# One ScalarE table set for logarithm and exponential in a hybrid RWKV / SSD / attention backbone

## The chip, the cores and the metric

The kernel runs on one core of one Trainium2 chip. The time is the device time of one execution, in microseconds (us), and the figure for a kernel is the median over its runs. Engines are named as in the profile: PE is TensorE (PEld its weight loads), DVE is VectorE, ACT is ScalarE, POOL is GpSimd, SP is SyncE, which here only issues transfers. ACT computes a function by a table. The tables come in sets, one set is active at a time, and an instruction ACT_TABLE_LOAD makes another set the active one. A set holds several functions; if a function's set is not the active one, the compiler puts a load in front of the ACTIVATE that needs it.

## The reference, cut to what matters

Four layers over 256 context tokens and 256 latent tokens of width 1024. Layers 0 and 3 mix tokens by a bidirectional RWKV-7 scan, layer 1 by a bidirectional Mamba-2 SSD scan, layer 2 by windowed attention; each is followed by a gated convolutional FFN. All is float32.

```python
def rmsnorm(x, g, eps=NORM_EPS):
    xf = x.astype(jnp.float32)
    xf = xf * lax.rsqrt(jnp.mean(xf * xf, axis=-1, keepdims=True) + eps)
    return (xf * g.astype(jnp.float32)).astype(x.dtype)

for i in range(DEPTH):
    hl, hc = modulate(xl, norm1_g[i], ...), modulate(xc, norm1_g[i], ...)
    yc, yl = mixer(hc, hl, ...)             # rwkv, ssd, attention, rwkv
    xl = xl + ml[2] * yl                    # the same for xc, except after the last layer
    xl = xl + ml[5] * conv_ffn(modulate(xl, norm2_g[i], ...), ...)
return rmsnorm(xl, final_g)
```

A root of the form rsqrt(m + eps) is wanted at nine places: before every mixer (n10, n11, n12, n13 in the kernel), before every FFN (n20 to n23), and once at the end (nf). Inside the mixers there are more: in SSD one per group of 256 channels (`group_rmsnorm`, 8 groups), in RWKV two per tile of 128 channels (8 tiles in each of the two layers), one that makes the key a unit vector (`kkf * rsqrt(sum(kkf * kkf) + 1e-12)`) and one in the head norm of the output. SSD and RWKV need plain exponentials besides (decays), SSD and the FFN need SiLU, RWKV needs sigmoid.

## The kernel before

Each engine has its own program, and semaphores tie them. ACT has no reciprocal root that is used here: every root is exp(-0.5 ln(m + eps)), an ACTIVATE with Ln and one with Exp.
The order of work on each engine is the order in which the program is written; nothing reorders it later. The stages that the change touches:

- Norms taken by halves of the tokens (`half_norm_act`, L659 to L674; tags n20, n11, n21, n12, n22, n23). PE computes the mean square of the first half (L588, L591) while it still ends the second half of the stage before. ACT takes the root (L669 Ln, L670 Exp), DVE multiplies X by it (L681), ACT or DVE scale and shift (L673, L683) into H, and PE goes on with the next stage's products on H (L649, or L884 in the FFN). Then all again for the second half, with `table(act, LOGS)` in front.
- Norms in one piece (`inverse_root`, L714 to L717): n10 at the very start, n13 before layer 3, nf at the end. DVE L775 (L748 in nf) and ACT L734 follow, and before an RWKV layer DVE L782 and L785, which form the token-shift mixes that PE L258 multiplies.
- The start of an FFN: after n2x, DVE forms differences of token halves (L988 to L991) and sums of weight blocks (L1004 to L1007), and PE L884 multiplies them.
- SSD, 8 groups: per group ACT loads EXPS (L2078), takes exponentials of the decays (L2059, L2055, L2042), then the root of the group before (`scale`, L2062 to L2066), more exponentials, loads SILUS and does convolutions' SiLU (L2008). DVE L2205 applies the root. POOL multiplies by the decays (L1807, L1813).
- RWKV, 8 tiles: in a long list of small 64x64 products on PE (L2419), copies out of PSUM are made by ACT (L2676) and DVE (L2981, L2989). Between them `slot_steps` places the next tile's element work: "TS" loads the sigmoid set, "L01" and "L23" are the sigmoids, "TL" loads LOGS, "KS" is the Ln for the key, "TE" loads EXPS, "KE" the Exp for the key; "P2" (L2783, Ln) and "P2e" (L2786, Exp) are the root of the head norm of an earlier tile.

Of the kernel before, what the change touches and what calls it, by code (L numbers as in the profile page):

```python
# [35 lines left out]
ORDER_Q = [[0, 1, 2, 3, 4, 5, 6, 7], [3, 2, 1, 0, 7, 6, 5, 4]]  # L36
LEVELS = (2, 4, 8, 16, 32)

EXPS, SIGMOIDS, LOGS, SILUS = 0, 2, 5, 18  # L39
HEADS = 16  # L40
SSD_IN = 6208
INNER = 2048
# [91 lines left out]
def program(nc, a, out, draft, scratch, layers=range(DEPTH), mixers=True, only=range(DEPTH)):  # L134
    C = Counts(draft)
    ctx = ExitStack()
    with ctx:
# [52 lines left out]
        pe, act, vec, pool, sp = nc.tensor, nc.scalar, nc.vector, nc.gpsimd, nc.sync  # L190
# [7 lines left out]
        def leave(own, stage):  # L198
            for s in own:
                C.end(s, stage)  # L200
# [11 lines left out]
        def table(act, functions):  # L212
            act.add_instruction(mybir.InstLoadActFuncSet(name=nc.get_next_instruction_name(), act_func_set_id=functions))  # L213

        def s(ins, label=None, i=None):

            ins.then_inc(act_done, C.mark(act_done, label))
            act.wait_ge(act_done, C.here(act_done, i))
# [360 lines left out]
        def halves(tag):  # L579

            if tag in ("n23", "mo3"):
                return ((slice(SEG, SEG + P), 1), (slice(SEG + P, T), 1))
            return ((SEGS[0], 0), (SEGS[1], 1))
# [75 lines left out]
        def half_norm_act(tag, prev, gain, shift):  # L659
            table(act, LOGS)  # L660
            act.wait_ge(vec_done, C.ended(vec_done, f"{prev}.front"))
            if C.ended(pool_done, prev) > 0:
                act.wait_ge(pool_done, C.ended(pool_done, prev))
            for n in range(2):
                o, sample = halves(tag)[n]
                if n:
                    table(act, LOGS)
                act.wait_ge(pe_done, C.at(f"{tag}.ms{n}"))
                s(act.activation(RS[:, o], PS[:, MS_BANK, o], ACT.Ln, bias=MC[:, 0:1]))  # L669
                s(act.activation(RS[:, o], RS[:, o], ACT.Exp, scale=-0.5), f"{tag}.rs{n}")  # L670
                for k in BY_ACT:
                    act.wait_ge(vec_done, C.at(f"{tag}.t{k}{n}"))
                    s(act.activation(Hk[:, k, o], TMP[k][:, o], ACT.Identity, scale=MS[:, gain, k, sample:sample + 1],  # L673
                                     bias=shift(k, sample)), f"{tag}.h{k}{n}")  # L674
            leave((act_done,), tag)
# [1081 lines left out]
        TE = WORK[:, 10240:10272].rearrange("p (d c e) -> p d c e", d=2, c=NCH)  # L1757
# [554 lines left out]
        def slot_steps(h):  # L2312

            i, s = h // 2, h % 2
            chain = [(k, 2 * ((h - 1) // 2) + d, 4 * ((h - 1) % 2) + c) for c in range(4) for k in "WUS" for d in range(2)]
            chain = chain if h else []
            if h == SLOTS:

                steps, at = [], {1: "P1", 5: "P2", 7: "P2e", 11: "P2v", 13: "P3"}
                for n, step in enumerate(chain):  # L2320
                    steps.append(step)
                    if n in at:
                        steps.append((at[n], i - 2))
                    if n % 2:
                        steps.append(("O", n // 12, n // 2 % 6, n // 2 % 6 + 1))
                return steps + [("YE", i - 1), ("O", 2, 0, 3), ("P1", i - 1), ("O", 2, 3, 6), ("P2", i - 1)] + [
                    ("O", m, 6, 7) for m in range(3)] + [("P2e", i - 1), ("O", 3, 0, 4), ("P2v", i - 1), ("P3", i - 1),
                                                         ("O", 3, 4, 7)]
            both = (2 * i, 2 * i + 1)
            inv = [("G", both[0], s), ("G", both[1], s), ("R", i, s), ("H", both[0], s)]  # L2330
            for m in range(len(LEVELS)):
                inv += [(k, q, s, m) for k in "ZX" for q in both]
                if m == 0:
                    inv.append(("H", both[1], s))

            beside = []
            if s == 0:
                if i + 1 < KD:
                    beside += [(k, n, i + 1) for k, n in (
                        (2, "kf"), (5, "TS"), (10, "L01"), (12, "L23"), (13, "sc0"), (14, "TL"), (14, "KS"), (16, "sub0"),  # L2340
                        (17, "sc1"), (18, "TE"), (22, "KE"), (24, "sub1"))]
                if i >= 2:
                    beside += [(k, n, i - 2) for k, n in ((15, "P1"), (17, "P2"), (20, "P2e"), (21, "P2v"), (23, "P3"))]
            elif i + 1 < KD:
                beside += [(k, n, i + 1) for k, n in (
# [3 lines left out]
            beside.append((5, "Rv", i, s))  # L2349
            if h + 1 < SLOTS:  # L2350
                beside += [(22 + d, "I", 2 * ((h + 1) // 2) + d, (h + 1) % 2) for d in range(2)]
            steps = [("I", d, 0) for d in range(2)] if h == 0 else []
            for k, step in enumerate(inv):
                steps.append(step)
                if k < len(chain):
                    steps.append(chain[k])
                steps += [b[1:] for b in beside if b[0] == k]
            if s == 0 and i:
                steps.append(("YE", i - 1))
            return steps  # L2360
# [15 lines left out]
        def run(steps):  # L2376

            for q in range(SLOTS + 1):
                for kind, *at in slot_steps(q):
                    if kind in steps:  # L2380
                        steps[kind](*at)
# [290 lines left out]
        def rwkv_act(l, lo):  # L2672
# [50 lines left out]
            def pn(n, d):  # L2723
                act.wait_ge(vec_done, C.at(f"{t}.t{n}.sums{d}"))
                s(act.activation(PN[:, d, :], ARS[:, d, 1, :], ACT.Exp, scale=LOG_W, bias=MC[:, 3:4]), f"{t}.t{n}.pn{d}")
# [8 lines left out]
            def ax(n, d):  # L2734
                s(act.activation(ARS[:, d, :, :], ARS[:, d, :, :], ACT.Exp, scale=-LOG_W, bias=MC[:, 2:3]),
                  f"{t}.t{n}.ax{d}")
# [48 lines left out]
            def post2e(j):  # L2785
                s(act.activation(RSB[:, lo:T], RSB[:, lo:T], ACT.Exp, scale=-0.5), f"{t}.t{j}.rs")  # L2786

            staging = {"TS": lambda n: table(act, SIGMOIDS), "TL": lambda n: table(act, LOGS),
                       "TE": lambda n: table(act, EXPS),
                       "kf": kf, "L01": l01, "L23": l23, "KS": ks, "KE": kse, "pn0": lambda n: pn(n, 0), "pn1": lambda n: pn(n, 1), "pct": pct, "ax0": lambda n: ax(n, 0),  # L2790
                       "ax1": lambda n: ax(n, 1), "pr1a": lambda n: replacement(n, 0),
                       "pr1b": lambda n: replacement(n, 1), "VT": vt}
# [391 lines left out]
```

## Time and profile before

| what | value |
|---|---|
| median of 3 runs | 3761.34 us (3756.88 to 3764.07) |
| the profiled execution's own time | 3758.67 us |
| its span | 3756.9 us |
| PE busy | 3635.3 us, 97% |
| DVE busy | 2692.6 us, 72% |
| ACT busy | 1462.2 us, 39% |
| POOL busy | 313.1 us, 8% |
| table loads on ACT | 127 instructions |

The span runs from the first to the last instruction; the execution's own time is 1.8 us more. A busy share is of the span. PE is busy nearly all the time, so what can be won by other engines' work lies in the places where PE stands still. Such a place has a row with a number in square brackets: the idle time of the engine just before the instruction, and what ended it.

### The profile page before, as it was taken

Reading aid. Unit: us, or ns where it says so; the run is one execution under the profiler, and the core shown is the slowest. Engines: PE = TensorE matmul, PEld = TensorE weight load, DVE = VectorE, ACT = ScalarE, POOL = GpSimd, SP = SyncE. Lnnn points to the kernel's source line nnn. Section 1 sums busy time; section 2 is a strip of 40 time slices with the busy share of each in tenths; the row PEclk is TensorE's granted clock in tenths of the full one; section 3 lists DMA queues with packets and bytes.
Section 4 is the critical chain, followed back from the end, with each engine's and each line's share of the span. In section 5 each row is a group of like instructions: output and inputs, shape, how many; then the busy total and the mean of one; then the engine's idle time right before and its main releaser. Section 6 shows DMA issues by size and latency. Waiting matters only on the chain.

```text
span 3756.9 us, 86184 instructions
## 1 busy us (share of the span) xinstructions
PE 3635.3 (97%) x34789; PEld 2689.0 (72%) x34789; DVE 2692.6 (72%) x4800; ACT 1462.2 (39%) x2799; POOL 313.1 (8%) x273
## 2 busy tenths in 40 slices
PE   6999999999999999999999999999998999999998
PEld 2448888688877454555887866588874568888887
DVE  7888778479998666663898944489977767776431
ACT  4036776333302545541332024233302157775211
POOL 2011101000000323220000000000001000010000
PEclk8999999999999999999999999999999999999999
DMA  6640000044343333223443520144443610000454
GB/s 199 199 137 4 4 4 15 22 135 127 124 151 98 102 96 104 79 77 99 129 128 119 168 62 26 41 134 133 131 122 106 202 38 4 4 4 15 120 151 132
DMA packets 481448, 351.38 MB, mean 94 GB/s; under 512 B 25280, under 2 KB 450568, under 8 KB 478888
## 3 DMA queue, kind: packets, MB, share of 16 engines
q1 hardware_dynamic: 454632, 235.94, 21.7%
q0 software_dynamic: 26432, 110.07, 8.3%
q8 instruction: 272, 4.46, 0.5%
q14 instruction: 112, 0.92, 0.1%
HBM read 344.76 MB, written 1.18 MB: 92 GB/s over the span
## 4 chain that ended last, share of the span: by engine, by line
PE 77%; DVE 13%; ACT 6%; issue 2%; DMA 1%; POOL 0%; DVEq 0%; SPq 0%; ACTq 0%; POOLq 0%
PE PS L884 21%; PE PS L258 17%; PE PS L2419 15%; PE PS L1413 8%; PE PS L1158 5%; PE PS L1523 2%; PE PS L611 2%; DVE WORK L535 1%; PE PS L1571 1%; DVE WORK L2151 1%; DVE WORK L2154 1%; ACT WORK L2676 1%; PE PS L1893 1%; PE PS L1583 1%; DVE WORK L2178 1%
## 5 line engine op out<-in xcount | busy, mean ns | idle before, releaser
L2419 PE MATMUL PS<-WORK 64*64 64x64 f32 (+2 forms) x13088 | 568.6, 224 | 14.8 <-ACT WORK L2676 6.0
L2419 PEld LDWEIGHTS PS<-WORK 64*64 64x64 f32 (+1 forms) x13088 | 478.2, 136 | 88.9 <-ACT WORK L2676 27.7
L258 PE MATMUL PS<-H,WR 128*128 128x512 f32 (+1 forms) x1424 | 477.0, 494 | 0.0
L535 DVE SCALAR_TENSOR_TENSOR WORK<-WORK,SC 128x512 f32<-128x512 f32 x616 | 419.3, 747 | 0.9
L258 PEld LDWEIGHTS PS<-H,WR 128*128 128x128 f32 x1424 | 268.0, 190 | 187.2 <-issue 165.9
L1413 PE MATMUL PS<-BIG,WR 128*128 128x512 f32 (+1 forms) x944 | 329.0, 502 | 5.8 <-DMA WR<-in_rw_wo_dram 2.5
L2676 ACT ACTIVATE WORK<-PS 128x256 f32<-128x256 f32 (+3 forms) x720 | 244.2, 339 | 228.4 <-PE PS L2419 210.7
L951 ACT ACTIVATE WORK<-PS 128x512 f32<-128x512 f32 x252 | 137.1, 544 | 367.5 <-PE PS L884 361.4
L1413 PEld LDWEIGHTS PS<-BIG,WR 128*128 128x128 f32 x944 | 176.1, 190 | 134.0 <-issue 113.1
L884 PE MATMUL PS<-BIG 128*128 128x256 f32 x984 | 223.9, 380 | 0.0
L515 POOL DMA_DIRECT2D WORK<-in_ada_w_dram x88 | 66.3, 753 | 1880.7 <-DVE WORK L535 818.2
L258 PE MATMUL PS<-WORK,WR 128*128 128x512 f32 (+1 forms) x544 | 211.7, 545 | 1.4 <-DMA WR<-in_rw_wr_dram 1.4
L884 PEld LDWEIGHTS PS<-BIG 128*128 128x128 f32 x984 | 186.0, 190 | 25.1
L884 PE MATMUL PS<-BIG,WORK 128*128 128x256 f32 x792 | 176.6, 379 | 5.0 <-issue 5.0
L884 PE MATMUL PS<-H,BIG 128*128 128x256 f32 x768 | 178.1, 380 | 0.8 <-ACT H L673 0.7
L258 PEld LDWEIGHTS PS<-WORK,WR 128*128 128x128 f32 x544 | 102.0, 190 | 101.5 <-issue 88.7
L1032 DVE SCALAR_TENSOR_TENSOR WORK<-WORK,PV 128x510 f32<-128x510 f32 x252 | 172.2, 743 | 3.1 <-ACT WORK L962 3.0
L884 PEld LDWEIGHTS PS<-BIG,WORK 128*128 128x128 f32 x792 | 150.2, 190 | 26.4 <-issue 6.1
L258 PE MATMUL PS<-BIG,WR 128*128 128x512 f32 (+1 forms) x320 | 147.0, 612 | 22.1 <-DVE BIG L785 22.1
L2419 PE MATMUL PS<-BIG,WORK 64*64 64x64 f32 x1920 | 149.3, 229 | 16.5 <-DVE WORK L2989 7.1
L884 PEld LDWEIGHTS PS<-H,BIG 128*128 128x128 f32 x768 | 145.2, 190 | 23.0 <-ACT H L673 3.5
L2981 DVE COPY_PREDICATED WORK<-K,PS 128x128 f32<-128x128 int32 x320 | 104.1, 325 | 69.1 <-PE PS L2419 59.7
(357 smaller groups left out, 6369.8 us busy)
## 6 DMA issues: line engine op xcount, KB each, us to landing
WORK<-in_ada_w_dram POOLq DMA_DIRECT2D x88, 1024.0 KB, 6.8
WR<-in_ffn_w_in_dram SPq DMA_DIRECT2D x220, 256.0 KB, 2.9
BIG<-in_ffn_w_in_dram SPq DMA_DIRECT2D x132, 256.0 KB, 3.3
WR<-in_ffn_w_out_dram SPq DMA_DIRECT2D x106, 256.0 KB, 2.9
WR<-in_ssd_w_in_dram SPq DMA_DIRECT2D x96, 256.0 KB, 2.9
BIG<-scratch_dram POOLq DMA_DIRECT2D x8, 2048.0 KB, 7.9
BIG<-in_ffn_w_out_dram SPq DMA_DIRECT2D x36, 256.0 KB, 3.3
BIG<-in_ada_w_dram SPq DMA_DIRECT2D x4, 2048.0 KB, 18.3
```

Of the source, the lines that this page charges most:

```text
L258: mm = pe.matmul(outs, WR[:, slot, k, 0:m], rhs(k), start=first and k == 0, stop=last and k == nk - 1)
L535: lag(vec.scalar_tensor_tensor(ACC3[:, s_], w, by, ACC3[:, s_], ALU.mult, ALU.add), label)
L611: mm = pe.matmul(PS[:, HALF_BANKS[tag][m][n], o], WR[:, slots[j], k, :], rhs(8 * r + k)[:, o], start=r == 0 and k == 0, stop=r == r_last a ...
L884: mm = pe.matmul(out, lhs(k), rhs(k), start=start and k == 0, stop=stop and k == 3)
L951: s(act.activation(EV[f % 2][:, n0:n0 + n, :], ps[:, 0:n, :], ACT.Copy), lab(f, "e" + bank))
L1032: lag(vec.scalar_tensor_tensor(dst, whole[h][:, :, t // 2:SEG - 1 + t // 2], tap(t, h, f), dst, ALU.mult, ALU.add), lab(f, "cv") if (t, h) ...
L1158: mm = pe.matmul(PS[:, bank, SEGS[n]], lhs(k), rhs(k), start=(r, n, k) == (0, 0, 0), stop=(r, n, k) == (PARTS - 1, 0 if alone else 1, nk - 1))
L1413: mm = pe.matmul(PS[:, bank, lo:T], WR[:, opened[label], k, :], rhs(8 * r + k), start=r == 0 and k == 0, stop=last and k == nk - 1)
L1523: mm = pe.matmul(PS[:, bank, :], WR[:, slot, k, :], Hk[:, k, :], start=k == 0, stop=k == KD - 1)
L2419: return pe.matmul(o, lhs, rhs, start=start, stop=stop)
L2676: s(act.activation(dst, src, ACT.Copy), f"{t}.{label}")
L2981: v(vec.copy_predicated(y, level.bitcast(mybir.dt.int32), PS[:, 3 + d, 4 * Q:4 * Q + P].rearrange("p (c k n) -> p c k n", c=4, n=n)), f"{t ...
```

## The change

```diff
-EXPS, SIGMOIDS, LOGS, SILUS = 0, 2, 5, 18
+EXPS, SIGMOIDS, LOGS, SILUS = 6, 2, 6, 18
...
             for n in range(2):
                 o, sample = halves(tag)[n]
-                if n:
-                    table(act, LOGS)
                 act.wait_ge(pe_done, C.at(f"{tag}.ms{n}"))
...
-                        (17, "sc1"), (18, "TE"), (22, "KE"), (24, "sub1"))]
+                        (17, "sc1"), (22, "KE"), (24, "sub1"))]
...
             staging = {"TS": lambda n: table(act, SIGMOIDS), "TL": lambda n: table(act, LOGS),
-                       "TE": lambda n: table(act, EXPS),
```

The programs of PE, DVE, POOL and SP stay as they are, instruction for instruction. ACT's has 62 table loads where it had 127; no other instruction of it moves. Three lines are gone from the file, so that an instruction below them in the file has a line number smaller by two or three.

ACT's program at the norm n20, from the last root of layer 0's mixer to the start of the FFN, before:

```order
L2786 ACT_TABLE_LOAD
L2786 ACTIVATE WORK<-WORK 128x512
L213 ACT_TABLE_LOAD
L669 ACTIVATE WORK<-PS,MC 128x256
L670 ACT_TABLE_LOAD
L670 ACTIVATE WORK<-WORK 128x256
L673 ACTIVATE H<-WORK,MOD,MS 128x256 x5
L213 ACT_TABLE_LOAD
L669 ACTIVATE WORK<-PS,MC 128x256
L670 ACT_TABLE_LOAD
L670 ACTIVATE WORK<-WORK 128x256
L673 ACTIVATE H<-WORK,MOD,MS 128x256 x5
```

and with the change:

```order
L2784 ACTIVATE WORK<-WORK 128x512
L213 ACT_TABLE_LOAD
L667 ACTIVATE WORK<-PS,MC 128x256
L668 ACTIVATE WORK<-WORK 128x256
L671 ACTIVATE H<-WORK,MOD,MS 128x256 x5
L667 ACTIVATE WORK<-PS,MC 128x256
L668 ACTIVATE WORK<-WORK 128x256
L671 ACTIVATE H<-WORK,MOD,MS 128x256 x5
```

One load goes from the first half's root and two from the second half's; the one at the head of the norm stays, although the set is active already.

ACT's program in an RWKV tile of layer 0, from the load of LOGS to the Exp for the key (L2721), before:

```order
L213 ACT_TABLE_LOAD
L2718 ACTIVATE WORK<-PS,MC 128x512
L2779 ACTIVATE WORK<-WORK 128x512
L2768 ACTIVATE WORK<-WORK 128x64
L2676 ACTIVATE WORK<-PS 128x256
L2768 ACTIVATE WORK<-WORK 128x64
L2783 ACTIVATE WORK<-PS,MC 128x512
L2676 ACTIVATE WORK<-PS 128x256
L2676 ACTIVATE WORK<-PS 128x64
L213 ACT_TABLE_LOAD
L2676 ACTIVATE WORK<-PS 128x64
L2786 ACTIVATE WORK<-WORK 128x512
```

and with the change:

```order
L213 ACT_TABLE_LOAD
L2716 ACTIVATE WORK<-PS,MC 128x512
L2777 ACTIVATE WORK<-WORK 128x512
L2766 ACTIVATE WORK<-WORK 128x64
L2674 ACTIVATE WORK<-PS 128x256
L2766 ACTIVATE WORK<-WORK 128x64
L2781 ACTIVATE WORK<-PS,MC 128x512
L2674 ACTIVATE WORK<-PS 128x256
L2674 ACTIVATE WORK<-PS 128x64 x2
L2784 ACTIVATE WORK<-WORK 128x512
```

The load between the two 128x64 copies out of PSUM is gone, nothing else.

ACT's program at the final norm nf, before:

```order
L213 ACT_TABLE_LOAD
L716 ACTIVATE WORK<-PS,MC 128x256
L717 ACT_TABLE_LOAD
L717 ACTIVATE WORK<-WORK 128x256
L734 ACTIVATE H<-WORK,MS 128x256 x5
```

and with the change:

```order
L213 ACT_TABLE_LOAD
L714 ACTIVATE WORK<-PS,MC 128x256
L715 ACTIVATE WORK<-WORK 128x256
L732 ACTIVATE H<-WORK,MS 128x256 x5
```

The load between Ln and Exp is gone; the one ahead of the Ln stays, since SiLU was active before.

## Rows read from the trace of the kernel before

**Rows 1.** The page: busy us of each engine (share of the span), instructions.

```profile
PE 3635.3 (97%) x34789; PEld 2689.0 (72%) x34789; DVE 2692.6 (72%) x4800; ACT 1462.2 (39%) x2799; POOL 313.1 (8%) x273
```

**Rows 2.** Groups by line, ACT: count | busy us, mean ns | idle before, releaser.

```profile
L213 ACT ACT_TABLE_LOAD x81 | 103.9, 1283 | 4.5 <-DVE BIG L785 2.7 <-ACT WORK L1321 0.2
L670 ACT ACT_TABLE_LOAD x12 | 15.4, 1283 | 0.2
```

**Rows 3.** Waits of PE: us in total, times, longest us.

```profile
PE PS L2419 <- ACT WORK L2676: 9.9, 26, 1.0
PE PS L884 <- issue: 5.0, 3, 1.7
```

**Rows 4.** Timeline, n20 to the FFN: start, us, instruction [idle before <-releaser].

```profile
771.82 1.28 ACT L670 ACT_TABLE_LOAD   x1
...
773.63 1.34 DVE L681 TENSOR_TENSOR WORK<-X,WORK 128x256 f32<-128x256 f32 x3 [3.59 <-ACT WORK L670]
...
785.88 0.69 DVE L1007 TENSOR_TENSOR WORK<-BIG,WORK 128x512 f32<-128x512 f32 x1
786.67 5.42 PE L884 MATMUL PS<-BIG,WORK 128*128 128x256 f32 x24 [1.66 <-issue]
...
788.85 0.69 DVE L1004 TENSOR_TENSOR BIG<-WR 128x512 f32<-128x512 f32 x1 [2.29 <-DMA WR<-in_ffn_w_in_dram]
```

**Rows 5.** Timeline, n13 to the first product of layer 3.

```profile
2870.00 1.28 ACT L717 ACT_TABLE_LOAD   x1
...
2872.02 2.14 DVE L775 TENSOR_TENSOR WORK<-X,WORK 128x512 f32<-128x512 f32 x3 [3.62 <-ACT WORK L717]
...
2875.92 2.05 PE L258 MATMUL PS<-BIG,WR 128*128 128x512 f32 x2 [6.75 <-DVE BIG L785]
```

**Rows 6.** Timeline, the final norm nf.

```profile
3743.65 1.28 ACT L717 ACT_TABLE_LOAD   x1
...
3746.66 2.94 PE L1456 MATMUL PS<-K,H 128*128 128x128 f32 x10 [3.62 <-ACT H L734]
```

**Rows 7.** Timeline of PE, second halves of n11, n12 and n23.

```profile
1195.86 5.36 PE L649 MATMUL PS<-H,WR 128*64 128x256 f32 x22 [0.29 <-ACT H L673]
...
2196.33 5.22 PE L649 MATMUL PS<-H,WR 128*128 128x256 f32 x22 [0.24 <-ACT H L673]
...
3514.79 2.07 PE L649 MATMUL PS<-H,WR 128*128 128x128 f32 x10 [0.60 <-ACT H L673]
...
3517.19 3.03 PE L649 MATMUL PS<-H,WR 128*128 128x128 f32 x22 [0.32 <-ACT H L673]
```

**Rows 8.** Timeline of PE, RWKV of layers 0 and 3: its waits on ACT.

```profile
504.88 0.77 PE L2419 MATMUL PS<-WORK 64*64 64x64 f32 x20 [0.16 <-ACT WORK L2676]
...
666.25 1.82 PE L2419 MATMUL PS<-WORK 64*64 64x32 f32 x56 [0.99 <-ACT WORK L2676]
...
3432.59 1.82 PE L2419 MATMUL PS<-WORK 64*64 64x32 f32 x56 [0.77 <-ACT WORK L2676]
...
3467.53 0.59 PE L2419 MATMUL PS<-WORK 64*64 64x64 f32 x8 [0.49 <-ACT WORK L2676]
...
3485.68 0.70 PE L2419 MATMUL PS<-WORK 128*128 128x256 f32 x2 [0.61 <-ACT WORK L2786]
```

**Rows 9.** Timeline, SSD, from the exponentials of one group to its state products.

```profile
1307.10 9.48 POOL L1813 TENSOR_TENSOR BIG<-BIG,WORK 128x2048 f32<-128x2048 f32 x2 [4.64 <-ACT BIG L2055]
1307.17 5.02 DVE L2151 TENSOR_TENSOR WORK<-BIG,WORK 128x512 f32<-128x512 f32 x1
1309.88 1.28 ACT L2065 ACT_TABLE_LOAD   x1
1311.18 0.69 ACT L2065 ACTIVATE WORK<-PS,MC 128x512 f32<-128x512 f32 x1
1317.16 0.69 DVE L2151 TENSOR_TENSOR WORK<-BIG,WORK 128x512 f32<-128x512 f32 x1
1317.22 0.63 ACT L2042 ACTIVATE WORK<-WORK 128x512 f32<-128x512 f32 x1 [2.61 <-DVE WORK L2154]
```

## The prediction

> **What bounds the kernel now.** I read the busy times first. PE is busy 3635.3 us, 97% of the span, and ACT 1462.2 us, 39% [rows 1]. So the change takes time from an engine that has much to spare, and the question is only how much of it PE stood and waited for. Next the groups by line, for the price of what goes: a table load takes 1283 ns, in all of the 81 at L213 and the 12 at L670 [rows 2]. Then PE's waits: on the copies L2676 of ACT it stands 9.9 us over 26 times, and there is one entry of 5.0 us in 3 times put down to "issue" [rows 3]. With these lists in hand I went to the timeline of each stage that has a removed load, and looked for the next idle time of PE behind it, and for who was the last to be waited for. The reader is to see there that most loads lie in time that ACT had free, that some sit on a chain ACT to DVE to PE, and that the idle of PE at the end of such a chain is shorter than the loads: that idle, not the load, is what can be won.
>
> **What is removed.** 127 loads become 62, so 65 go: 65 x 1.283 us = 83.4 us of ACT's busy time [rows 2]. Nothing is added and no instruction of another engine moves. By place the 65 are: 12 + 6 in the six half norms (one in a first half, two in a second), 3 in n10, n13 and nf, 16 in the roots of SSD, 14 "TE" of RWKV, and 14 that the compiler had put at roots of RWKV. What each place is worth:
>
> - *Start of the FFN in layers 0, 1 and 2.* In the second half of n20 the load of LOGS and the one at 771.82 stand between the end of the first half's work and the root; DVE L681 waits 3.59 us for it and starts at 773.63. From there DVE works almost without a break to L1007, which ends at 786.57, and PE, idle for 1.66 us, starts at 786.67 [rows 4]. Both loads gone, the root is 2.57 us earlier (the mean square had been ready, so ACT alone was late), DVE has that idle time to give, and L1007 ends some 2.57 us earlier, before PE wants it. So the idle of 1.66 us goes whole and 0.9 us of the shift is left over. Three such places make the 5.0 us of the "issue" entry [rows 3]: 3 x 1.66 = 4.98 us. What comes next there: DVE L1004 waits for a transfer until 788.85 [rows 4], and that will not be earlier, since it was issued before the gap; but its sums are for the block after, which PE reaches some 10 us later. I count no new wait.
> - *n13.* ACT L717's load at 2870.00 is followed by Exp, DVE L775 (idle 3.62 us for it) and the chain to PE, which is idle for 6.75 us [rows 5]. PE has nothing else: the whole 1.28 us.
> - *nf.* The same at 3743.65, PE idle 3.62 us [rows 6], and only stores behind it: 1.28 us. n10: its root is ready long before DVE needs it, at the start of the program: 0.
> - *Second halves of n11, n12, n23.* Two loads, 2.57 us, before H; but PE has products of the first half to do and idles only 0.29 us, 0.24 us, and in n23 0.60 and 0.32 us [rows 7]. All of these go: 1.45 us. First halves: there DVE waits for PE's last product of the stage before, or is busy with it, so that one load less buys nothing.
> - *"TE" in RWKV.* The load stands between two copies out of PSUM, and PE is idle for 0.16 us behind it at 504.88 [rows 8], five times in layer 0, so 0.8 us of 7 x 1.28. In layer 3, where the outputs of the context tokens are left out and DVE leads, I find no idle of PE behind "TE": 0.
> - *Roots in the tails of RWKV*, where no sigmoids are between: behind a load at L2783 PE is idle for 0.99 us in layer 0, and in layer 3 for 0.77, 0.49 and 0.61 us [rows 8]: 2.86 us. Elsewhere in the tails PE has big products to do: 0.
> - *SSD, 16 loads of 20.5 us.* The load at 1309.88 is followed by the Ln and Exp, and then ACT has 2.61 us to wait anyway, until 1317.22, for DVE [rows 9]. DVE is late because its L2151 takes 5.02 us while POOL runs L1813 for 9.48 us, against 0.69 us at 1317.16 without it. ACT's exponentials that start POOL stand ahead of the removed loads, so that this stays. The last group's root has PE's products of other channels beside it. So 0.
>
> Sum: 4.98 + 1.28 + 1.28 + 1.45 + 0.80 + 2.86 = 12.65 us. Against the profiled execution: 3758.67 - 12.65 = 3746.0 us. The median of the runs shown is 2.7 us above that execution; against it the forecast is 3761.34 - 12.65 = 3748.7 us.
>
> **The bounds.** Lower end of the gain: only what stands directly before an idle PE with nothing between (n13, nf, tails, second halves, "TE"), without the FFN starts: 7.7 us, 3753.7. Upper end: PE's ends of products are modelled, so a gap may be larger than it looks. Taken at the full length of the loads at the FFN starts (3 x 2.57) and at the five "TE" (5 x 1.28), the gain grows by 2.7 + 5.6 us, to 20.9 us, 3740.4. I take the idle times as shown, since the waits of PE are what the trace measures nearest to the question.
>
> **A rule to weigh.** The loads and their neighbours stand back to back in this trace: the load at 1309.88 lasts to 1311.16 and the Ln starts at 1311.18 [rows 9]. The Trainium skill, "ScalarE: Activation LUTs", section "What ACT_TABLE_LOAD costs", gives as measured about 1283 ns for the load and about 1380 ns more for a drain, some 2.66 us for every switch to another set. The trace agrees with the first number and shows no room for the second. With 1380 ns more at n13 and at nf the sum would be about 15.4 us by that page.
>
> **The rivals.**
> - *A. The gain is given back at once.* PE runs into a DVE or ACT result of the next block sooner. Against it: behind the FFN start PE shows no further idle; for it: DVE's chain in the FFN is long, and in RWKV 9.9 us of waits on L2676 are mostly not behind loads [rows 3]. If the FFN starts (4.98) and the RWKV terms (3.66) go elsewhere, 4.0 us are left: 3757.3 us.
> - *B. More than the idle.* In the tiles of RWKV the chain itself turns through ACT, and 1.28 us less in it brings all that follows forward: the upper end above, 3740.4 us.
> - *C. Slower: POOL and DVE meet.* In SSD a DVE instruction beside POOL's takes 5.02 in place of 0.69 us [rows 9]. POOL's work in RWKV starts from exponentials of ACT. If ACT, being earlier, moved POOL onto a DVE instruction that PE waits for, at each of 14 tiles twice, and each cost a fifth of the difference of 4.33 us (an estimate: POOL's pieces there are shorter), that is 28 x 0.87 = 24 us: 3773 us. It decides from 15 such meetings on, where the 12.65 us are used up. Against it: those exponentials wait for DVE's running sums and not for the load, so that the two keep their places to each other.
> - *D. It doesn't do what it says.* If the set that holds both functions had to be loaded again, the loads would stand in ACT's program, and they do not. If its Ln or Exp ran slower, the elements would take the time that the loads gave back; ACT has 61% free for that [rows 1], but on the chains above it would count. With nothing won: 3761 us.
> - *E. A load holds ACT up for longer than its record,* as much again, by something that the rows put into its neighbours. It would count where PE has idle time left for it, at n13 and nf [rows 5, 6]: 2 x 1.28 = 2.57 us more, 3746.1 us. Against it is the 0.02 us between a load and the next instruction [rows 9]. The rule above points this way.
>
> **Chances.** The forecast with its small errors 0.68; A 0.13; B 0.10; E 0.03; C 0.03; D with no gain 0.03. About 7.5 us, 0.2%, is what a measurement of this kernel can tell from no change, so faster is all below 3753.8: the forecast nearly whole (0.65 of 0.68), B, E, and some 0.02 of A: 0.80. Within 0.2%: the rest of A, of the forecast and D: 0.17. Slower: C, 0.03. Time 3748.7 us. The range reaches up to A's 3757 and down to 3742, most of the way to B: 3742 to 3757.
>
> **What would show it.** ACT's busy time down by 83 us to about 1379, and 62 loads. The "issue" wait of PE L884 gone from the list of waits; DVE L681 of n20's second half waiting about 1.0 in place of 3.59 us; PE's idle before L258 at n13 5.47 in place of 6.75 us, and before L1456 2.34 in place of 3.62 us; no idle of PE before L649 in second halves; PE's copies wait (L2676) at about 7 in place of 9.9 us. SSD's period from group to group, by DVE L2151's starts, unchanged. It is wrong if PE shows new idle behind the FFN starts, if SSD gets shorter, or if the tiles of RWKV get shorter by over 0.2 us each.

## The result, and the profile after

With the change the kernel takes 3741.61 us (median of 6 runs, 3737.57 to 3744.11), beside 3760.86 us for the kernel before on the same chip (3756.88 to 3764.25, 6 runs). The ratio is 0.9948, with an interval of 0.9936 to 0.996: 19.3 us faster. The forecast was 3748.7 us, a gain of 12.65 us; the time lies 0.4 us below the lower end of the range. The profiled execution took 3742.13 us where 3746.0 was forecast, with a span of 3740.3 us, 16.6 us shorter than before. So the direction and the order of size were right, and the gain was half as large again as forecast.

The page after, busy us of each engine (share of the span) and instructions:

```profile
PE 3628.7 (97%) x34789; PEld 2688.1 (72%) x34789; DVE 2692.5 (72%) x4800; ACT 1377.9 (37%) x2734; POOL 312.0 (8%) x273
```

Against [rows 1], ACT is busy 84.3 us less with 65 instructions fewer, and PE 6.6 us less with the same number of products. That second difference was not forecast: idle time that goes does not shorten a product. It is the first sign of a part of the gain that the idle column doesn't show.

The group of loads after. 61 of the 62 stand under one line now; the other, L401, is in both kernels:

```profile
L213 ACT ACT_TABLE_LOAD x61 | 78.3, 1283 | 4.1 <-DVE BIG L783 2.7 <-ACT WORK L1319 0.2
```

PE's waits after, in the columns of [rows 3]; line numbers behind the norms are 2 or 3 lower than before:

```profile
PE PS L258 <- DVE BIG L783: 19.0, 14, 7.7
...
PE PS L2417 <- ACT WORK L2674: 7.5, 19, 0.7
PE PS L2417 <- DVE WORK L2986: 7.4, 21, 0.5
...
PE PS L649 <- ACT H L671: 2.1, 3, 1.0
```

The "issue" entry of [rows 3] is gone, and the waits on ACT's copies are down from 9.9 us in 26 to 7.5 us in 19.

The start of the first FFN, which answers to [rows 4]:

```profile
769.17 1.35 DVE L679 TENSOR_TENSOR WORK<-X,WORK 128x256 f32<-128x256 f32 x3 [1.02 <-ACT WORK L668]
...
781.42 0.69 DVE L1005 TENSOR_TENSOR WORK<-BIG,WORK 128x512 f32<-128x512 f32 x1
782.95 3.40 PE L882 MATMUL PS<-BIG,WORK 128*128 128x256 f32 x15
```

DVE waits 1.02 us for the root where it had waited 3.59. The vector L1005 is done at 782.11 and PE starts on it at 782.95, with no idle before it: DVE is now 0.84 us ahead, where the forecast had 0.9.

The start of layer 3, which answers to [rows 5]:

```profile
2861.12 2.14 DVE L773 TENSOR_TENSOR WORK<-X,WORK 128x512 f32<-128x512 f32 x3 [2.34 <-ACT WORK L715]
...
2865.01 2.05 PE L258 MATMUL PS<-BIG,WR 128*128 128x512 f32 x2 [5.47 <-DVE BIG L783]
...
3729.50 0.44 PE L1454 MATMUL PS<-K,H 128*128 128x128 f32 x2 [2.35 <-ACT H L732]
```

The last row is the final norm's and answers to [rows 6]. PE's idle is 5.47 in place of 6.75 us, and 2.35 in place of 3.62: 1.28 and 1.27 us, one load at each place.

SSD, which answers to [rows 9]:

```profile
1302.44 9.46 POOL L1811 TENSOR_TENSOR BIG<-BIG,WORK 128x2048 f32<-128x2048 f32 x2 [4.65 <-ACT BIG L2053]
1302.51 5.02 DVE L2149 TENSOR_TENSOR WORK<-BIG,WORK 128x512 f32<-128x512 f32 x1
...
1312.54 0.63 ACT L2040 ACTIVATE WORK<-WORK 128x512 f32<-128x512 f32 x1 [4.67 <-DVE WORK L2152]
```

POOL and DVE meet as before, with the same 5.02 us, and ACT waits 4.67 us for DVE where it had waited 2.61. From the POOL row to the ACT row it is 10.10 us, and was 10.12. The time that the two loads held is idle time of ACT now.

### The profile page after: what moved, and what is told of

Its sections match the earlier page's. It is cut to its first block, busy times and chain, and to the rows that moved or that the text cites. A ratio compares the mean times of both kernels' runs of the same rounds, so it can differ in the third digit from the quotient of the medians.

```text
span 3740.3 us, 86139 instructions
## 1 busy us (share of the span) xinstructions
PE 3628.7 (97%) x34789; PEld 2688.1 (72%) x34789; DVE 2692.5 (72%) x4800; ACT 1377.9 (37%) x2734; POOL 312.0 (8%) x273
## 4 chain that ended last, share of the span: by engine, by line
PE 70%; DVE 18%; ACT 6%; issue 3%; DMA 1%; SPq 1%; DVEq 0%; POOL 0%; ACTq 0%; POOLq 0%
PE PS L258 17%; PE PS L882 15%; PE PS L2417 15%; PE PS L1411 8%; PE PS L1156 4%; DVE WORK L535 2%; PE PS L1521 2%; PE PS L611 2%; DVE WORK L1030 1%; PE PS L1569 1%; DVE WORK L2149 1%; DVE WORK L2152 1%; ACT WORK L2674 1%; PE PS L649 1%; PE PS L1891 1%
## 5 line engine op out<-in xcount | busy, mean ns | idle before, releaser
L882 PE MATMUL PS<-BIG 128*128 128x256 f32 x984 | 223.9, 380 | 0.0
L882 PEld LDWEIGHTS PS<-BIG 128*128 128x128 f32 x984 | 186.0, 190 | 25.1
L882 PE MATMUL PS<-H,BIG 128*128 128x256 f32 x768 | 178.1, 380 | 0.8 <-ACT H L671 0.7
L882 PE MATMUL PS<-BIG,WORK 128*128 128x256 f32 x792 | 176.3, 379 | 0.0
L882 PEld LDWEIGHTS PS<-BIG,WORK 128*128 128x128 f32 x792 | 150.5, 190 | 20.5
L882 PEld LDWEIGHTS PS<-H,BIG 128*128 128x128 f32 x768 | 145.2, 190 | 23.0 <-ACT H L671 3.5
```

The lines of the kernel that those rows point to most:

```text
L882: mm = pe.matmul(out, lhs(k), rhs(k), start=start and k == 0, stop=stop and k == 3)
```

## What was tested

My theory after the result was that the gain comes from the four kinds of place that the prediction names (FFN starts and second halves, the norms n13 and nf, the tails of RWKV, a little at "TE"), and that each is worth more than the idle that the trace shows. The rivals were B (most of the excess comes from "TE"), E (a load costs more than its record, so n13 and nf give 2.57 us more), something in SSD after all, and the chance that PE's clock differs between executions. e2, e3, e4, e6 and e9 each put the loads of one kind of place back into the changed kernel. They name the set that is active already; each still takes its 1.28 us. The expectations weigh two theories of the tails of RWKV: "stalls only", PE gains the waits that go and nothing else, and "clock", behind such a wait PE's granted clock falls for a while, and the change spares it that as well. Some numbers below are "by the starts": the same product of PE is looked up in two traces, and what lies between two such products is compared. Below, "loses" is against the changed kernel of the same call.

**e1: the changed kernel again, as the measure for the next three.** No edit.

> The changed kernel once more, beside the kernel before and the kernels with one part of the change undone. Both theories expect 17 to 20 us less than before. It also tells how far its trace repeats: theory 'clock' (part of the gain is that PE, no longer idle in the tail of layer 3, keeps its full granted clock there) expects no stretch of lower clock between 3415 and 3450 us; theory 'stalls only' has no word on it.

Measured: 3741.26 us (3738.33 to 3747.17), ratio 0.9944 (0.9931 to 0.9958). The gain stands: 20.3 us by the medians. Its profiled span was 3745.4 us, 5.1 more than the first profile of the same instructions, so single profiles of this kernel differ by a few us.

**e2: the 18 loads in the half norms back.**

```diff
                 o, sample = halves(tag)[n]
+                if n:
+                    table(act, LOGS)
                 act.wait_ge(pe_done, C.at(f"{tag}.ms{n}"))
                 s(act.activation(RS[:, o], PS[:, MS_BANK, o], ACT.Ln, bias=MC[:, 0:1]))
+                table(act, EXPS)
                 s(act.activation(RS[:, o], RS[:, o], ACT.Exp, scale=-0.5), f"{tag}.rs{n}")
```

> The change with the 18 loads of the six half norms put back (one in a first half, two in a second). By the prediction's count (idle of PE as the timeline shows it: 4.98 + 1.45 us) it loses 6.4 us of the gain. By the comparison of the two traces, where PE's product starts in the second halves are late by more than the rows show as idle (1.9 us at each of three FFN starts, some 0.8 in n11, 1.5 in n12, 1.0 in n23), it loses 9.0 us.

Measured: 3750.94 us (3748.53 to 3755.9), ratio 0.9972 (0.9961 to 0.9982). It loses 9.7 us; the forecast had 4.98 + 1.45 = 6.4 us for these places. The timeline of PE at the start of the first FFN shows how much is at one of them:

```profile
771.51 13.98 PE L885 MATMUL PS<-H,WR 128*128 128x256 f32 x64
787.15 5.42 PE L885 MATMUL PS<-BIG,WORK 128*128 128x256 f32 x24 [1.66 <-issue]
```

and the same 64 products with the change:

```profile
769.14 13.98 PE L882 MATMUL PS<-H,WR 128*128 128x256 f32 x64
```

From the start of the 64 to the start of what follows it is 787.15 - 771.51 = 15.64 us here and 782.95 - 769.14 = 13.81 us with the change. The difference is 1.83 us (1.90 with what lies just ahead of the 64), and the idle shown is 1.66. The reason is in the rows: 64 products in 13.81 us start 0.216 us apart, while the record of one lasts 0.379 us (the median of L882's). The records overlap, and the last of a chain ends 0.16 us after the time at which a next product could have started. So an idle of PE behind such a product is shown 0.16 us too short, and one shorter than that isn't shown at all. The Trainium skill, "Perfetto Trace Analysis", section "Tensor Engine Instruction (MATMUL, LD_WEIGHTS)", says that the end of a product is estimated from its size and not observed. This trace agrees in so far as the shortest, the median and the longest of these products all have 0.379 us. That the records overlap by 0.16 us is measured here, and how much of it is the estimate isn't shown.

How much a hidden wait can be is seen at n12. PE's products before, in the second half of n12:

```profile
2188.23 7.87 PE L649 MATMUL PS<-H,WR 128*128 128x256 f32 x32
```

and with the change:

```profile
2181.61 11.82 PE L649 MATMUL PS<-H,WR 128*128 128x256 f32 x54
2193.26 1.02 PE L1532 MATMUL PS<-BIG 128*128 128x512 f32 x2
```

Before, 32 products take from 2188.23 to 2196.33 [rows 7], 0.253 us each; after, 54 take from 2181.61 to 2193.26, 0.216 us each. Of 32 x 0.216 = 6.9 us the 8.1 us before are 1.2 us too many, in waits of which only the last shows as 0.24 us; with the small ones ahead of it PE gained 1.5 us at n12, where the prediction counted 0.24. By the starts in e2's own trace its loads cost 5.7 us at the FFN starts, 0.8 in n11, 1.5 in n12 and 3.3 in n23, against e1. What is special about n23 is seen in e8 below.

**e3: the loads at roots in the tails of RWKV back.**

```diff
                 act.wait_ge(pe_done, C.at(f"{t}.t{j}.va"))
+                if j >= 5:
+                    table(act, LOGS)
                 s(act.activation(RSB[:, lo:T], PS[:, 6, lo:T], ACT.Ln, bias=MC[:, 1:2]))
 
             def post2e(j):
+                if j >= 5:
+                    table(act, EXPS)
                 s(act.activation(RSB[:, lo:T], RSB[:, lo:T], ACT.Exp, scale=-0.5), f"{t}.t{j}.rs")
```

> The change with the 12 loads at the roots of the RWKV tails put back (tiles 5 to 7 of layers 0 and 3). By the prediction's count (0.99 + 0.77 + 0.49 + 0.61 us) it loses 2.9 us. Theory 'clock' expects the stretch of granted clock 0.5 between 3434 and 3442 us of the kernel before to be back, with some 2.6 us of slower products in it: it loses 5 to 6 us.

Measured: 3749.0 us (3745.51 to 3754.63), ratio 0.9965 (0.9951 to 0.9979). It loses 7.7 us, where 2.86 were forecast. The 0.16 us is not enough for that: by the starts of PE's products in the two first traces the four waits of [rows 8] without "TE" are worth 1.15, 0.94, 0.58 and 0.77 us, in sum 3.4 us, and with small ones close behind them 4.1 us. The timeline of e3 in the tail of layer 0 shows the rest:

```profile
665.91 1.28 ACT L213 ACT_TABLE_LOAD   x1 [0.85 <-PE PS L2417]
...
668.36 1.82 PE L2417 MATMUL PS<-WORK 64*64 64x32 f32 x56 [0.99 <-ACT WORK L2674]
...
670.49 0.48 PE L2417 MATMUL PS<-WORK,BIG 64*64 64x64 f32 x4 [0.31 <-DVE WORK L2990]
```

Two windows of e3 there (stretch and length in us, then for PE, PEld, DVE, ACT and POOL the busy us and instructions, the granted clock, DMA share, GB/s):

```profile
666.00:670.00 4.00, 3.01 (x104) 2.88 (x100) 1.12 (x3) 3.87 (x6) 0.00 (x0) 1.00 0.01 4
670.00:677.50 7.50, 7.19 (x104) 5.46 (x102) 3.50 (x9) 3.31 (x9) 0.00 (x0) 0.54 0.01 3
```

and the kernel before over the same products, which it reaches 2.1 us sooner:

```profile
667.90:675.40 7.50, 7.08 (x174) 5.87 (x172) 5.62 (x14) 3.94 (x11) 0.00 (x0) 1.00 0.01 3
```

Behind the wait of 0.99 us the granted clock is 0.54, which is nearly all of the stretch at the lower level, 1.2 GHz; the four products at 670.49 take 0.48 us where they take 0.33 in the kernel before. In 7.5 us PE does 104 products and not 174. The kernel before stood here just as long (0.99 us, [rows 8]) and kept 1.00, but it had such a stretch in the tail of layer 3, behind the wait of 0.77 us at 3432.59:

```profile
3424.00:3434.00 10.00, 9.23 (x289) 8.69 (x287) 5.08 (x15) 6.74 (x16) 0.00 (x0) 1.00 0.02 4
3434.00:3442.00 8.00, 7.69 (x139) 6.81 (x137) 3.88 (x11) 3.76 (x11) 0.00 (x0) 0.57 0.02 4
```

The same place with the change, and a later one:

```profile
3424.00:3432.00 8.00, 7.69 (x222) 7.29 (x224) 5.41 (x15) 3.54 (x10) 0.00 (x0) 1.00 0.01 2
...
3477.00:3486.00 9.00, 9.00 (x40) 7.72 (x39) 3.95 (x10) 0.00 (x0) 0.00 (x0) 0.81 0.45 131
```

The stretch cost the kernel before 2.8 us, more than the wait ahead of it (the rows for this are with e8). In e3's trace there are two, at 670 and at 3432 us, and they cost 2.5 and 3.0 us by the starts. The 2.8 us are a part of the 6.6 us that PE is busy less; hidden waits, which count as busy, are another. The last row shows that the change doesn't rid the kernel of such stretches; it has a shorter one elsewhere.

**e4: the "TE" load of each tile back.**

```diff
-                        (17, "sc1"), (22, "KE"), (24, "sub1"))]
+                        (17, "sc1"), (18, "TE"), (22, "KE"), (24, "sub1"))]
...
             staging = {"TS": lambda n: table(act, SIGMOIDS), "TL": lambda n: table(act, LOGS),
+                       "TE": lambda n: table(act, EXPS),
```

> The change with the 14 steps 'TE' put back in the RWKV tiles. By the prediction's count (5 idles of 0.16 us) it loses 0.8 us. By the comparison of the traces, where 0.3 us won at the product behind the load is given back 20 products later, it loses 0.3 us or less. Rival B of the prediction (the chain turns through ACT) expects 5 us or more.

Measured: 3741.02 us (3740.35 to 3743.12), ratio 0.9946 (0.9933 to 0.996): 0.2 us less than e1, no difference. PE's row at this place with the load:

```profile
507.44 0.77 PE L2417 MATMUL PS<-WORK 64*64 64x64 f32 x20 [0.15 <-ACT WORK L2674]
```

The wait of [rows 8] is back and the time is not longer. The 0.3 us that it costs at the product (0.15 and the hidden 0.16) are nearly all made up 20 products later, where PE waits for DVE's results. A little stays: from 304 us to the tail of layer 0 the three profiles with the "TE" loads (before, e8, e4) take 358.8 to 358.9 us, and the nine without them 358.3 to 358.5. So "TE" is worth some 0.4 us in the traces, which the whole time can't show, and rival B, which wanted 5 us or more, is out.

**e5: one load in the tails back, in the one tile behind which the kernel before had its slow stretch.** Does one wait of 0.77 us bring the stretch along?

```diff
                 act.wait_ge(pe_done, C.at(f"{t}.t{j}.va"))
+                if (l, j) == (3, 5):
+                    table(act, LOGS)
                 s(act.activation(RSB[:, lo:T], PS[:, 6, lo:T], ACT.Ln, bias=MC[:, 1:2]))
```

> The change with a single load put back: the one between PE's product and the Ln of tile 5's head norm in the tail of layer 3, where PE of the kernel before is idle for 0.77 us. Theory 'stalls only' expects PE's product behind it to be 0.8 to 0.95 us later and nothing else. Theory 'clock' expects, behind that idle, the stretch of granted clock 0.5 of the kernel before (6.8 us from 3434.5) and 2.6 us more, so 3.4 us in all; since the stretches do not stand at the same place in each execution, it may be there in one profile and not in the next, and the median shift lies between 0.8 and 3.4 us.

Measured: 3743.09 us (3740.13 to 3744.71), ratio 0.9954 (0.994 to 0.9968), beside 3760.07 for the kernel before in this call. The timeline of e5:

```profile
3420.11 1.28 ACT L213 ACT_TABLE_LOAD   x1 [0.42 <-PE PS L2417]
...
3422.34 1.82 PE L2417 MATMUL PS<-WORK 64*64 64x32 f32 x56 [0.77 <-ACT WORK L2674]
...
3424.47 0.48 PE L2417 MATMUL PS<-WORK,BIG 64*64 64x64 f32 x4 [0.31 <-DVE WORK L2988]
```

and a window behind it, in e5:

```profile
3424.00:3431.00 7.00, 6.69 (x106) 5.81 (x103) 3.03 (x9) 2.10 (x6) 0.00 (x0) 0.52 0.01 2
```

and at the same time with the change:

```profile
3424.00:3431.00 7.00, 6.69 (x188) 6.29 (x190) 5.13 (x13) 2.71 (x8) 0.00 (x0) 1.00 0.01 2
```

In the profiled execution the stretch came with the load, in the tile where it was put. By the medians it is 1.8 us above e1 and 4.4 above e6 of the same call, where its wait of PE is worth 0.94 us; the intervals of all three overlap, so that the whole time doesn't settle what one load costs. By the starts in its trace the load costs 1.0 us at the wait and 2.9 behind it.

**e6: the 16 loads of SSD's roots back.**

```diff
+                table(act, LOGS)
                 s(act.activation(RSG, PS[:, 7, :], ACT.Ln, bias=MC[:, 0:1]))
+                table(act, EXPS)
                 s(act.activation(RSG, RSG, ACT.Exp, scale=-0.5), f"s{n}.rs")
```

> The change with the 16 loads of the SSD roots put back, 20.5 us of ACT's time. All theories expect no difference (below 0.5 us) from the changed kernel, since ACT waits for DVE behind them by 2.6 us as it is: the group's period stays 57.2 us. A longer period would speak for a chain through ACT that the prediction missed.

Measured: 3738.66 us (3736.71 to 3739.32), ratio 0.9944 (0.993 to 0.9958), the same ratio as e1's. SSD is worth 0, as forecast; the profile's rows of SSD above say why.

**e7: the change, and five channel blocks of the next norm's first half ahead, in place of three.** The second half of n11 still has idle time of PE. With the change:

```profile
1179.94 0.48 DVE L686 SCALAR_TENSOR_TENSOR X<-PS,MOD,X 128x256 f32<-128x256 f32 x1 [1.52 <-PE PS L611]
...
1182.10 1.08 PE L649 MATMUL PS<-H,WR 128*64 128x256 f32 x4 [0.83 <-ACT H L671]
```

DVE waits 1.52 us for a product of PE, and PE then 0.83 us for what DVE and ACT do behind it. DVE could do two more blocks of the first half in that time.

```diff
-                    half_norm_vec(f"n1{l + 1}", 0, range(3), 2 * l + 2, mod_shift(l + 1, 0))
+                    half_norm_vec(f"n1{l + 1}", 0, range(5), 2 * l + 2, mod_shift(l + 1, 0))
                     vec.wait_ge(w_used, C.at(f"fo{l}.w{m}2.used"))
                     add_half(m, 1, PS[:, HALF_BANKS[f"fo{l}"][m][1], :], l, 5, f"fo{l}")
-                    half_norm_vec(f"n1{l + 1}", 0, range(3, KD), 2 * l + 2, mod_shift(l + 1, 0))
+                    half_norm_vec(f"n1{l + 1}", 0, range(5, KD), 2 * l + 2, mod_shift(l + 1, 0))
```

> The change and, beyond it, five in place of three channel blocks of H made before PE's last product in the first halves of n11 and n12 (DVE has 1.5 us free there since the load is gone). PE's idle of 0.83 us (n11) and 0.98 us (n12) before its fourth block should go: 1.6 to 2.2 us less than the change, some 3739.5 us.

Measured: 3735.41 us (3734.78 to 3741.33), ratio 0.9939 (0.9924 to 0.9953). The same rows in e7:

```profile
1180.78 2.37 PE L649 MATMUL PS<-H,WR 128*64 128x256 f32 x10
...
1180.97 0.48 DVE L686 SCALAR_TENSOR_TENSOR X<-PS,MOD,X 128x256 f32<-128x256 f32 x1 [0.16 <-PE PS L611]
```

PE's idle of 0.83 us is gone at n11, and so is that at n12. By the starts it is 1.04 and 1.23 us, 2.3 us in the trace. It is the fastest kernel of the study, 3.3 us below e6 of the same call and 24.7 us below the kernel before, but the intervals of e6 and e7 overlap; only the 2.3 us is shown.

**e8: one more look at the kernel before,** for its clock in the tails. No edit.

> The kernel before once more, one look, for its trace. Theory 'clock' expects stretches of granted clock below 1 in the tails of RWKV (near 666 or 3434 us) again, behind PE's idle there; 'stalls only' has no word on it.

Measured: one time, 3757.66 us, span 3755.9 us. The stretch at half clock in layer 3's tail is missing in this profile (granted clock 1.00 in the last 70 us of RWKV, 0.95 in the first profile). So the same instructions stand here with and without it. The kernel before, from the wait to a product behind the stretch:

```profile
3432.59 1.82 PE L2419 MATMUL PS<-WORK 64*64 64x32 f32 x56 [0.77 <-ACT WORK L2676]
...
3442.22 0.28 PE L2419 MATMUL PS<-WORK 64*64 64x64 f32 x4
```

and e8:

```profile
3434.70 1.82 PE L2419 MATMUL PS<-WORK 64*64 64x32 f32 x56 [0.77 <-ACT WORK L2676]
...
3441.53 0.28 PE L2419 MATMUL PS<-WORK 64*64 64x64 f32 x4
```

That is 9.63 us and 6.83 us: the stretch costs 2.8 us. The span of e8 is only 1.0 us shorter all the same, since the earlier part of layer 3's RWKV, where stretches come and go, took 3.0 us longer in it. So the span of a single profile doesn't price the stretch. Without it the loads in the tails cost PE 4.1 us by the starts, e8 against e1.

e8 also corrects a row that the prediction read. At n23 the kernel before shows PE waiting 0.60 us for the second half's H [rows 7]:

```profile
3503.56 2.84 PE L611 MATMUL PS<-BIG,WR 128*128 128x128 f32 x24
...
3510.16 4.03 PE L649 MATMUL PS<-H,WR 128*128 128x128 f32 x22
```

The same wait in e8:

```profile
3508.97 3.02 PE L649 MATMUL PS<-H,WR 128*128 128x128 f32 x22
3513.78 2.07 PE L649 MATMUL PS<-H,WR 128*128 128x128 f32 x10 [1.79 <-ACT H L673]
```

and the place with the change:

```profile
3490.38 2.84 PE L611 MATMUL PS<-BIG,WR 128*128 128x128 f32 x24
...
3496.62 4.32 PE L649 MATMUL PS<-H,WR 128*128 128x128 f32 x32
3501.27 3.02 PE L649 MATMUL PS<-H,WR 128*128 128x128 f32 x22 [0.32 <-ACT H L671]
```

In the kernel before a stretch at half clock covered the 22 products ahead of the wait (granted clock 0.85 from 3510 to 3520 us). They took 4.03 us in place of 3.02 and so filled most of the wait, which is 1.79 us in e8. The stretch cost nothing there, since what PE waited for came no later: from the 24 products of L611 to the last 22 of L649 (3517.19, [rows 7]) it is 13.63 us, and 13.62 in e8. With the change it is 10.89. So n23 is worth 2.7 us, where the prediction counted 0.92.

**e9: the three loads in n10, n13 and nf back.**

```diff
                 s(act.activation(RS[:, lo:T], PS[:, 0, lo:T], ACT.Ln, bias=MC[:, 0:1]))
+                table(act, EXPS)
                 s(act.activation(RS[:, lo:T], RS[:, lo:T], ACT.Exp, scale=-0.5), f"{tag}.rs")
```

> The change with the 3 loads of the norms in one piece put back (n10, n13, nf; between Ln and Exp). Both theories expect 2 x 1.28 = 2.6 us less gain, PE idle 6.75 us before layer 3's first product and 3.62 us before the last transposes, as in the kernel before. If a load held ACT for as much again (rival E), it would be 5.1 us.

Measured: 3742.92 us (3741.09 to 3743.64), ratio 0.9941 (0.9928 to 0.9955), beside 3764.37 for the kernel before in this call, which ran on another chip. The final norm in e9:

```profile
3728.09 1.28 ACT L213 ACT_TABLE_LOAD   x1
...
3731.10 2.94 PE L1455 MATMUL PS<-K,H 128*128 128x128 f32 x10 [3.63 <-ACT H L733]
```

PE's idle is 3.63 us again, 1.28 more than the 2.35 with the change: one load, and not two. By the whole times the 2.6 us of this edit don't show, since the ratio is as good as e1's; calls differ by more than that. Rival E asked for 5.1 us. Since e9's loads name the set that is active already, the switch to another set is shown by the first two traces: there the load between Ln and Exp did change the set, and its going took 1.28 and 1.27 us off PE's idle.

**e10: e3's kernel again,** in the call of e9, since e3 carried the largest surprise. The edit is e3's.

> The 12 tail loads put back once more, to see whether the loss of 7.7 us and the stretches of lower clock repeat. 'Stalls only' expects the 2.9 us of the prediction's count; 'clock' expects 5 to 8 us, and a stretch of granted clock 0.5 in at least one of the two tails (after 660 us in layer 0, after 3415 us in layer 3), but not surely in both.

Measured: 3747.61 us (3743.91 to 3751.1), ratio 0.9955 (0.9941 to 0.9968). It is 4.7 us above e9 of the same call, and would be some 7.3 above it without e9's own loads (2.6 us by its trace). By the ratio it is 0.0011 above e1, 4.1 us. With e3's 7.7 us the tails are worth 4 to 8 us, still more than the 2.86 forecast. The window over the tail of layer 0, in e10:

```profile
655.00:726.00 71.00, 69.19 (x1483) 53.59 (x1481) 31.77 (x83) 31.14 (x76) 0.00 (x0) 0.95 0.01 3
```

The granted clock is the same 0.95 in e3: both have the half-clock stretch at 670 us. In the tail of layer 3 e3 has one and e10 has none.

How the clock fell out over all profiles: of the five with a load ahead of the waits in the tails (before, e8, e3, e10, e5) four have a stretch at half clock behind one of them, and e8 has none. Counted by waits (those of 0.99 us in layer 0 and 0.77 us in layer 3), it is five of nine. Of the seven without such a load (after, e1, e2, e4, e6, e7, e9) none has one there; only after has a short one later in the same tail, shown above at 3477. Each execution that was timed with a clock also lists its mean granted clock. Over 40 executions with loads in both tails (30 of the kernel before, and e3 and e10) the mean is 0.9912, and over 39 without any there (the changed kernel, e1, e2, e4, e6, e7, e9) it is 0.9929; e2 alone, with the loads of the norms, has 0.9928. Among executions of the same kernel one with 0.001 less takes some 1.9 us longer (a straight line through all that are listed); by it the 0.0017 are some 3 us, an estimate. So the lower clock goes with the loads in the tails, and not in the profiled executions alone.

Elsewhere in RWKV of layer 3 such stretches come and go between executions of one and the same kernel. That is where spans of equal kernels part; RWKV of layer 3 over the same products in e1:

```profile
3041.00:3414.00 373.00, 348.56 (x9452) 310.93 (x9453) 281.44 (x621) 253.52 (x568) 32.55 (x28) 0.98 0.02 4
```

and in e6, where the clock is full all along and the stretch 4 us shorter:

```profile
3036.00:3405.00 369.00, 343.99 (x9459) 305.36 (x9457) 282.02 (x623) 254.01 (x569) 32.98 (x28) 1.00 0.02 5
```

What is not settled: how much of the tails' 4 to 8 us is the clock in an average execution. The waits themselves are 4.1 us; the rest, up to 4 us, fits one stretch of 2.4 to 3.0 us in many executions, but only profiled executions list where the clock fell. Nor is it shown that the wait is what makes the clock fall. A kernel that fills the waits with products of no use, to keep the engine busy and leave the wait in, would tell. It wasn't tried.

## Why the prediction was right in direction and a third short

Step by step, with what each term came to (by the starts of PE's products before and after, and by the experiment that undoes it):

| step | forecast | by the traces | by the experiments |
|---|---|---|---|
| FFN starts, three | 4.98 | 3 x 1.90 = 5.7 | e2: 9.7 with the next |
| second halves n11, n12, n23 | 1.45 | 0.8 + 1.5 + 2.7 = 5.0 | in e2 |
| n13 and nf | 2.56 | 1.29 + 1.28 | e9: 2.6 in its trace |
| "TE" | 0.80 | 0.4 | e4: 0 |
| tails, waits | 2.86 | 4.1 | e3, e10: 4 to 8 with the next |
| tails, clock | not there | 2.8 | in e3, e10 |
| SSD | 0 | 0 | e6: 0 |
| sum | 12.65 | 17.8, and 20.6 with the clock | 16.3 to 20.3 |

The sum of the experiments (9.7 + 2.6 + 4 to 8) holds the 19.3 us between the medians, and so do the two sums of the traces, without and with one stretch in the tails. The sum with the clock is 4.0 us more than the 16.6 us between the two spans. Of these, 1.8 us by the starts are the changed kernel's own stretch at 3477, and 1.3 are RWKV of layer 3 ahead of its tail, which took that much longer in the changed kernel's profile; both differ as much between executions of one kernel (e1's profile lacks the first, and e8's second is 3.0 us longer than that of the kernel before). The last 0.9 is in small differences that I have not followed.

- **ACT's 65 loads and their price**: right. 1462.2 - 1377.9 = 84.3 us, with 83.4 forecast.
- **FFN starts**: right mechanism, and what was said would show it does (DVE's wait 1.02, the "issue" entry gone, 0.84 us left over). The term was mis-sized, 4.98 for 5.7.
- **n13, nf**: right to 0.01 us. With one load in front of an idle PE on both sides the 0.16 us falls out of the difference.
- **Second halves**: the step that failed most, 1.45 for 5.0 us, and with it the rule by which all the waits were priced. The sentence was "I take the idle times as shown, since the waits of PE are what the trace measures nearest to the question". PE's idle is what is left between modelled ends of products: at n12 0.24 us shown stood for 1.5. And one of the idles, the 0.60 us of n23, was short because a stretch at half clock in that one execution had filled it; 1.79 us is what e8 shows, and 2.7 us what n23 gave where 0.92 was counted. The bound named the reason ("a gap may be larger than it looks"), but put it at the FFN starts and "TE", up to the full length of the loads, and not at the small waits, where it is largest by ratio. "No idle before L649 in second halves" was wrong too for n23, where 0.32 us stays.
- **"TE"**: 0.8 for 0.4 by the traces and none by the whole time. The idle is real, but the next result PE waits for comes from DVE and is hardly earlier. That is rival A's mechanism, in one place.
- **Tails**: the waits were mis-sized, 2.86 for 4.1 us, and one thing was missing altogether: the kernel before ran at half clock behind a wait, in the very tail whose rows were read. A window over it shows the clock.
- **SSD and rival C**: right. DVE beside POOL takes 5.02 us as before.
- **Rival D** is out by the count of loads and the gain. **B** is out by e4 as to its mechanism; that its 3740.4 us lies only 1.2 us from the 3741.6 measured is luck. **E** is out by the first two traces and e9. As to E: the Trainium skill, "ScalarE: Activation LUTs", section "What ACT_TABLE_LOAD costs", has a drain of about 1380 ns beside the 1283 ns. This kernel doesn't show it: at n13 and nf together the loads' removal gave 2.57 us, where that rule would have 5.3.
- **Against the median**: the sum was worked out on one execution and set against the median. The execution before lay 2.2 us under its median in the comparison (3758.67, 3760.86), the one after 0.5 us over its own (3742.13, 3741.61). So 2.7 of the 6.65 us between 12.65 and 19.3 are the scatter of two single executions. The terms free of the clock came to 17.8 us, 5.1 more than the forecast; the clock in the tails is the likely rest.

## What to carry to other kernels

Price a removed wait by the starts of the products around it, not by the idle shown: take the spacing of the same products in an undisturbed chain (0.216 us here) times their number, and compare it with the time they took; this finds the waits that the idle column hides. Then look at the granted clock on both sides of the wait. Behind it, a stall of under 1 us was followed by 2.4 to 3.0 us of loss at five of nine waits here. Ahead of it, products at the lower clock fill the wait and make it look small: 0.60 us at n23 where a second profile of the same kernel had 1.79. And look for the next result that the engine waits for and ask whether it gets earlier as well: at "TE" it hardly did, and the gain was 0.4 us at most.

## What the runs showed of the hardware that I had not expected

- A wait of PE of 0.77 to 0.99 us, in chains of small products, was followed by a stretch at a granted clock of 0.5 (1.2 GHz) at five of nine such waits, in four of five profiles, at a cost of 2.4 to 3.0 us by the starts; at none of the same places in the seven profiles without the wait.
- A stretch at half clock ahead of a wait cost nothing: at n23 the 22 products took 4.03 in place of 3.02 us, the wait behind them was shown as 0.60 in place of 1.79, and the whole took 13.63 and 13.62 us.
- The record of a product of 128x256 lasts 0.379 us and the next starts after 0.216 us, so an idle of PE behind it is shown 0.16 us short; at n12 waits of 1.5 us showed as 0.24.
- The table load costs its 1.28 us and no more, also where an idle PE shows it (1.28 and 1.27 us at n13 and nf, and 1.28 put back in e9), and the exponential of the common set is as fast as that of its own: 0.629 us for 128x512 elements in both kernels' norms.
